# Projection stage of an encoder layer: x turned by the host, the RMS root applied to the output columns, two output buffers, tiles 0 and 1 multiplied while the weights arrive

## The chip, the cores and the metric

One NeuronCore of a Trainium2 chip. The metric is the time of one execution of the whole program on the device, in microseconds; lower is better. Work that the host does on the inputs before the launch is not in it.

## What is computed

A hybrid encoder layer in fp32 for 1024 + 512 tokens (12 tiles of 128), model width 1024: input projection, windowed attention (heads A), dense attention with normalised and rotated q and k (heads B), output projection, expert-choice mixture of 16 experts, a gated embedding. The change is in the first stage:

```python
def rmsnorm(x, g):
    xf = x.astype(jnp.float32)
    r = lax.rsqrt(jnp.mean(xf * xf, axis=-1, keepdims=True) + EPS)
    return (xf * r).astype(x.dtype) * g

h = rmsnorm(x, g_attn[i])
proj = h @ w_in[i]                       # (tokens, 1024) @ (1024, 1536)
qa, ka, va, qb, kb, vb = jnp.split(proj, splits, axis=-1)
# heads B: q = rope(rmsnorm(q, gq)), k = rope(rmsnorm(k, gk)), per head of 64
```

## The kernel before

`project_inputs` (L169) runs the stage; attention of the sample tiles follows. Every fp32 operand of a product is split into a high part (rounded to the PE's fp32r, by ScalarE, "ACT") and a low part (the remainder, by VectorE, "DVE"), and a product is three matmuls: high x high, high x low, low x high. The weights' 1536 columns are three chunks c of 512, held in one PSUM buffer `p_out` of three banks: chunk 0 and the first 128 columns of chunk 1 are q and k of heads B, then k of heads A, v of both, and chunk 2 is q of heads A. A tile is 3 chunks x 8 blocks of the depth x 3 = 72 matmuls of 512 columns.

Weights come in 8 blocks of 768 KB through a ring of three (`load_w`, L237), which waits for `w_lo_made` of three blocks before. ACT makes `w_hi` (L380), DVE `w_lo` (L482).

For each tile of x (512 KB): ACT squares and sums it (L330), GpSimd ("POOL") makes the root (L300 to L311), DVE multiplies x by root and by the gain row `g_all` (L417), PE turns it in eight 128 x 128 blocks into `p_xT` (L510), ACT and DVE split it (L336, L422). `p_xT` takes two PSUM banks, `p_qk` two, the bias rows `p_rows` one, `p_out` three: eight, which is all.

After a tile's products its columns are processed (`post_middle` and `post`): ACT squares q/k of B (L341) and copies v (L344) once chunk 1 is done, DVE sums per head (L433), POOL takes the power (L313, L315), DVE multiplies (L436), applies gains and rotation (L442 to L459), ACT and DVE split q and k (L351 to L360, L461 to L472). PE then turns them with the identity in six rounds of four 128 x 128 blocks (L553) into `p_qk` (two slots), ACT copies each round out (L373) to `qT` or `kT`, and SP's queue stores v, qT (1 MB) and kT (512 KB) in DRAM (L257 to L263). `qT` and `kT` have one buffer each: the first copy of a tile waits for `q_stored` of the tile before, the fifth for `k_stored`.

The order of each engine is written out by hand. PE, per tile t: chunk 0 of tile t - 1, turn x of tile t, chunk 1 of tile t - 1, two rounds of q turns of tile t - 2, chunk 2 of tile t - 1 with the other four rounds between its blocks. As `p_out` is one buffer, a chunk of tile t may begin only when DVE and ACT have read that chunk of tile t - 1:

```python
pe.wait_ge(dve_step, (t - 1) * V_STEPS + (V_NORM, V_KA_LO, V_QA_LO)[c])
if c == 1:
    pe.wait_ge(act_step, (t - 1) * A_STEPS + A_V)
```

Tile 0 is multiplied block by block while the weights arrive (`first_product`, L513), with chunk 1 to 3 of one block together; tile 1 follows after it.

The relative bias of heads A (`BiasRows`): PE looks the table up (L157) at the start, DVE adds (L161), and ACT issues one DMA (L166) after its last `w_hi`, which writes the eight rows 128 times, shifted, to `rel_d` in DRAM (2 MB, from 8 partitions). SP reads it back near the stage's end (`ahead.load_consts`).

SP's queue, per step: load x of a tile (waits until the slot is squared and normalised), then the three stores of the tile three before, each waiting for its copies.

Of the kernel before, what the change touches and what calls it, by code (L numbers as in the profile page):

```python
# [13 lines left out]
P = 128  # L14
# [125 lines left out]
class BiasRows:  # L140


    def __init__(self, a):
        self.table, self.hot = a.sb("table", [BUCKETS, HEADS]), a.sb("hot", [BUCKETS, REL])
        self.outside, self.rows = a.sb("outside", [HEADS, REL]), a.sb("rows", [HEADS, REL])
        self.p_rows = a.ps("p_rows", [HEADS, REL])
        self.landed, self.looked, self.added, self.stored = (
            a.sem(n) for n in ("bias_landed", "bias_looked", "bias_added", "bias_stored"))
# [20 lines left out]
def project_inputs(nc, kept, unit, x, w_in, g_attn, gqk, rope, rel_bias, hot, outside, qT_d, kT_d, v_d, rel_d, ahead):  # L169


    RING = 3
    with ExitStack() as ctx:
# [5 lines left out]
        g_all = sb("g_all", [P, D])  # L179
        gqk_s = sb("gqk_s", [P, 2, HD])  # L180
        nhalf = sb("nhalf", [P, HEADS + KV])
        eps = sb("eps", [P, HEADS + KV])
        x_sb = sb("x", [P, 2, D])
        cs = sb("cs", [P, TILES, 2 * HD])
        sq = sb("sq", [P, 2, D], mybir.dt.bfloat16)
        ss = sb("ss", [P, 2, 1])
        mean = sb("mean", [P, 2, 1])
        rinv = sb("rinv", [P, 2, 1])
        xn, xn_r = a.sb_both("xn", [P, 2, D])
# [25 lines left out]
        x_landed, cs_landed = sems("x_landed", 2), sem("cs_landed")  # L215
        squared, meaned, rooted, normed = sem("squared"), sem("meaned"), sem("rooted"), sem("normed")
        xT_made, h_hi_made, h_lo_made, mm_done = sem("xT_made"), sem("h_hi_made"), sem("h_lo_made"), sem("mm_done")
        act_step, dve_step, pool_step = sem("act_step"), sem("dve_step"), sem("pool_step")
# [9 lines left out]
        qkb, qa = p_out[:, 0:QK_B], p_out[:, 2 * BANK:QKV]  # L228
        ka = p_out[:, QK_B:QK_B + KV * HD]
        vba = p_out[:, QK_B + KV * HD:2 * BANK]  # L230
# [5 lines left out]
        def _(sp):  # L236
# [5 lines left out]
            sp.dma_start(x_sb[:, 0, :], x[0:P, :]).then_inc(x_landed[0], 16)  # L242
            sp.dma_start(g_all[:], g_attn.partition_broadcast(P)).then_inc(g_landed, 16)
            load_w(0)
            load_w(1)
            sp.dma_start(x_sb[:, 1, :], x[P:2 * P, :]).then_inc(x_landed[1], 16)
            load_w(2)
            bias.load(sp, rel_bias, hot, outside)
            sp.dma_start(gqk_all[:].rearrange("p a d -> p (a d)"), gqk.partition_broadcast(P)).then_inc(gqk_landed, 16)
            for k in range(3, KC):  # L250
                load_w(k)
# [13 lines left out]
            def load(t, s):  # L265
                row = sp.snap(t * P)
                sp.wait_ge(squared, t - 1)
                sp.wait_ge(normed, t - 1)
                sp.sem_inc(sp_turn, 1)
                sp.dma_start(x_sb[:, s, :], x[bass.ds(row, P), :]).then_inc(x_landed[s], 16)  # L270

            load(2, 0)
            sp.dma_start(cs[:], rope.rearrange("(t p) n -> p t n", p=P)).then_inc(cs_landed, 16)
            with sp.Fori(1, TILES // 2 - 1) as i:
                for k in range(2):
                    load(i * 2 + k + 1, 1 - k)
                    store(i * 2 + k - 2, k)
            load(TILES - 1, 1)
# [3 lines left out]
            store(TILES - 4, 0)  # L282
# [8 lines left out]
        def _(pool):  # L291
            unit.make(pool)
            pool.memset(nhalf[:], -0.5).then_inc(pool_step, 1)
            pool.memset(eps[:], EPS).then_inc(pool_step, 1)
            pool.wait_ge(pool_step, 2)


            for t in range(2):
                pool.wait_ge(squared, t + 1)
                pool.tensor_tensor(mean[:, t, :], ss[:, t, :], eps[:, 0:1], ALU.add).then_inc(meaned, 1)  # L300
                pool.wait_ge(meaned, t + 1)
                pool.tensor_tensor(rinv[:, t, :], mean[:, t, :], nhalf[:, 0:1], ALU.pow).then_inc(rooted, 1)
# [3 lines left out]

            def pair(t, s):
                pool.wait_ge(squared, t + 1)
                pool.tensor_tensor(mean[:, s, :], ss[:, s, :], eps[:, 0:1], ALU.add).then_inc(meaned, 1)
                pool.wait_ge(meaned, t * 2 - 1)  # L310
                pool.tensor_tensor(rinv[:, s, :], mean[:, s, :], nhalf[:, 0:1], ALU.pow).then_inc(rooted, 1)  # L311
                pool.wait_ge(dve_step, (t - 2) * V_STEPS + V_SUM)
                pool.tensor_tensor(meanh[:], ssh[:], eps[:], ALU.add).then_inc(meaned, 1)  # L313
                pool.wait_ge(meaned, t * 2)
                pool.tensor_tensor(rinvh[:], meanh[:], nhalf[:], ALU.pow).then_inc(pool_step, 1)  # L315

            with pool.Fori(0, TILES // 2 - 1) as i:
                for k in range(2):
                    pair(i * 2 + k + 2, k)
            for t in (TILES - 2, TILES - 1):  # L320
                pool.wait_ge(dve_step, t * V_STEPS + V_SUM)
                pool.tensor_tensor(meanh[:], ssh[:], eps[:], ALU.add).then_inc(meaned, 1)
                pool.wait_ge(meaned, TILES + t + 1)
                pool.tensor_tensor(rinvh[:], meanh[:], nhalf[:], ALU.pow).then_inc(pool_step, 1)

        @block.scalar
        def _(act):
            def square(t, s):
                act.wait_ge(x_landed[s], (t - s) * 8 + 16)
                act.activation(sq[:, s, :], x_sb[:, s, :], ACT.Square, scale=D ** -0.5, accum_out=ss[:, s, :]).then_inc(squared, 1)  # L330

            def high(t, s, first):
                act.wait_ge(xT_made, t + 1)
                if not first:
                    act.wait_ge(mm_done, (t - 1) * 3)
                act.activation(h_hi[:, s, :, :], p_xT[:], ACT.Copy).then_inc(h_hi_made, 1)  # L336

            def post_middle(t, s, second):

                act.wait_ge(mm_done, t * 3 + 2)  # L340
                act.activation(sqh[:], qkb, ACT.Square, scale=HD ** -0.5).then_inc(act_step, 1)  # L341
                if not second:
# [3 lines left out]
            def post(t, first):  # L346

                if not first:
# [3 lines left out]
                               ka.rearrange("p (h d) -> p h d", d=HD).unsqueeze(2).broadcast_to([P, KV, 2, HD]),  # L352
                               ACT.Copy).then_inc(act_step, 1)
                act.wait_ge(mm_done, t * 3 + 3)
                act.activation(q_hl[:, 0:HEADS, 0, :], qa.rearrange("p (h d) -> p h d", d=HD), ACT.Copy,
                               scale=SCALE).then_inc(act_step, 1)
# [1961 lines left out]
```

## Time and profile before

| | |
|---|---|
| median of 3 runs | 1571.12 us (1570.65 to 1572.77) |
| the profiled execution, its own time | 1573.29 us |
| its span, first to last instruction | 1571.5 us |
| PE busy | 1443.1 us (92%) |
| DVE, ACT, POOL busy | 932.7, 722.7, 180.0 us |
| mean granted clock of PE | 0.959 of full speed |
| the projection, until attention's first matmul | 0 to 274 us |

The profile gives, per engine, when each instruction began, how long it was busy and what ended the idle time before it. A matmul's busy time is longer than its share, since matmuls overlap: the distance between the starts of two of them is what one costs.

### The profile page before, as it was taken

How to read it: one execution, taken by the hardware profiler on the slowest of the kernel's cores; microseconds unless marked ns; L12 is line 12 of the kernel's file. 1: busy time of each engine (PE TensorE's matmuls, PEld its weight loads, DVE VectorE, ACT ScalarE, POOL GpSimd, SP SyncE). 2: the span in 40 equal slices, each digit the busy share in tenths (PEclk: the TensorE clock that was granted, in tenths of full speed). 3: DMA queues.
4: the chain of work that ended last, by engine and by line, in shares of the span. 5: the costliest groups of instructions: out<-in, count | busy, mean ns of one | idle time of the engine just before them, and what ended most of it. 6: DMA issues, size and time to landing. Idle time of an engine off the chain costs nothing. (4 is left out here: it accounts for less than half of the span.)

```text
span 1571.5 us, 21444 instructions
## 1 busy us (share of the span) xinstructions
PE 1443.1 (92%) x7320; PEld 1016.3 (65%) x7320; DVE 932.7 (59%) x1324; ACT 722.7 (46%) x1157; POOL 180.0 (11%) x240
## 2 busy tenths in 40 slices
PE   5899998899999889699998799999999999959997
PEld 4778887555566555378887556666666666637885
DVE  5444443667777677533256856776676776644544
ACT  4244433666677567522222544544544444433332
POOL 1111111000000000100001211121121121021110
PEclk9899999799999979899998889999999999979999
DMA  8533353511112243254342847788778778681331
GB/s 263 101 116 114 113 184 115 203 67 65 65 65 66 95 171 118 76 207 139 129 147 96 299 148 254 255 270 272 256 253 263 259 255 268 236 252 68 134 135 67
DMA packets 81983, 261.53 MB, mean 166 GB/s; under 512 B 7648, under 2 KB 37472, under 8 KB 66568
## 3 DMA queue, kind: packets, MB, share of 16 engines
q1 hardware_dynamic: 73728, 233.55, 41.4%
q0 software_dynamic: 7168, 25.17, 6.9%
q10 hardware_dynamic: 1032, 2.10, 1.2%
q8 instruction: 32, 0.52, 0.1%
q14 instruction: 23, 0.19, 0.0%
HBM read 194.20 MB, written 66.58 MB: 166 GB/s over the span
## 5 line engine op out<-in xcount | busy, mean ns | idle before, releaser
L1836 DVE TENSOR_TENSOR moe_w_lo<-ring,moe_w_hi 128x2048 fp32r<-128x2048 f32 x96 | 220.3, 2296 | 157.7 <-ACT moe_w_hi L1775 157.6
L1775 ACT ACTIVATE moe_w_hi<-ring 128x2048 fp32r<-128x2048 f32 x96 | 183.6, 1914 | 202.6 <-PE moe_p_g L1958 122.3
L1486 PE MATMUL mix_p_big<-kept_out_w,mix_m_hi 128*128 128x512 f32 x384 | 126.2, 410 | 4.6 <-DVE mix_m_lo L1361 2.4
L537 PE MATMUL proj_p_out<-proj_w_hi,proj_h_hi 128*128 128x512 f32 x264 | 110.4, 418 | 8.4 <-DVE proj_qn L436 8.4
L1966 PE MATMUL moe_p_gu<-ring,moe_xT_r 128*64 128x512 f32 x512 | 116.9, 598 | 0.0
L537 PE MATMUL proj_p_out<-proj_w_hi,proj_h_lo 128*128 128x512 f32 x264 | 105.3, 399 | 0.0
L537 PE MATMUL proj_p_out<-proj_w_lo,proj_h_hi 128*128 128x512 f32 x264 | 105.2, 399 | 0.0
L1034 DVE TENSOR_REDUCE sample_ntop<-sample_p_s 128x1 f32<-128x1024 f32 x64 | 78.2, 1223 | 42.0 <-PE sample_p_s L857 41.2
L871 PEld LDWEIGHTS sample_p_t<-kept_ident_r,sample_probs_r 128*128 128x128 f32 x688 | 73.0, 141 | 23.6 <-ACT sample_probs L972 6.6
L1486 PEld LDWEIGHTS mix_p_big<-kept_out_w,mix_m_hi 128*128 128x128 f32 x384 | 72.8, 195 | 21.4 <-issue 2.6
L871 PE MATMUL sample_p_t<-kept_ident_r,sample_probs_r 128*128 128x128 f32 x688 | 80.2, 246 | 5.0 <-ACT sample_probs L972 2.5
L2208 PE MATMUL tail_p_out<-kept_pg_hi,tail_h_hi 128*128 128x512 f32 x192 | 77.8, 405 | 2.4 <-DVE tail_h_lo L2152 2.4
L972 ACT ACTIVATE sample_probs<-sample_p_s,sample_ntop 128x1024 f32<-128x1024 f32 x64 | 71.5, 1117 | 18.1 <-DVE sample_ntop L1034 17.8
L1486 PE MATMUL mix_p_big<-kept_out_w,mix_m_lo 128*128 128x512 f32 x192 | 77.6, 404 | 0.0
L2208 PE MATMUL tail_p_out<-kept_pg_hi,tail_h_lo 128*128 128x512 f32 x192 | 76.9, 401 | 0.0
L1966 PEld LDWEIGHTS moe_p_gu<-ring,moe_xT_r 128*64 128x64 f32 x512 | 33.9, 136 | 66.1 <-issue 66.1
L2208 PE MATMUL tail_p_out<-kept_pg_lo,tail_h_hi 128*128 128x512 f32 x192 | 76.4, 398 | 0.0
L881 PE MATMUL sample_p_o<-sample_pT_b,sample_vb 128*64 128x512 f32 x256 | 62.9, 606 | 0.8 <-ACT sample_pT_b L959 0.8
L537 PEld LDWEIGHTS proj_p_out<-proj_w_hi,proj_h_hi 128*128 128x128 f32 x264 | 50.2, 190 | 17.7 <-issue 8.5
L1736 POOL DMA_INDIRECT acc_d<-ring,kept_slots x32 | 50.5, 1580 | 96.2 <-DVE ring L1877 91.9
L1966 PE MATMUL moe_p_yr<-ring,moe_hT_r 128*64 128x512 f32 x256 | 58.5, 598 | 0.0
L1725 POOL DMA_INDIRECT ring<-h_d,kept_slots x16 | 21.4, 1334 | 322.8 <-PE moe_p_t L1934 314.9
(303 smaller groups left out, 3154.7 us busy)
## 6 DMA issues: line engine op xcount, KB each, us to landing
ring<-in_w_gate SPq DMA_DIRECT2D x32, 1024.0 KB, 5.5
ring<-in_w_up SPq DMA_DIRECT2D x32, 1024.0 KB, 7.4
ring<-in_w_down SPq DMA_DIRECT2D x32, 1024.0 KB, 5.6
qT_d<-proj_qT SPq DMA_DIRECT2D x12, 1024.0 KB, 3.9
proj_x<-in_x SPq DMA_DIRECT2D x12, 512.0 KB, 4.8
proj_w_raw<-in_w_in SPq DMA_DIRECT2D x8, 768.0 KB, 6.1
kT_d<-proj_kT SPq DMA_DIRECT2D x12, 512.0 KB, 3.9
ahead_q<-qT_d SPq DMA_DIRECT2D x6, 1024.0 KB, 5.0
```

The costliest lines, as they stand in the source:

```text
L537: last = pe.matmul(p_out[:, cols], h[:, s, k, :], w[:, k, cols], start=(k == 0 and n == 0), stop=(k == KC - 1 and n == 2))
L871: last_mm = pe.transpose(p_t[:, bank, b, :].bitcast(F32R), probs_r[:, head % 4, at:at + P], ident_r[:])
L881: mm = pe.matmul(p_o[kv * HD:(kv + 1) * HD, :, :], v, pT[:, b, kv, :, :], start=(b == begin), stop=(b == end - 1))
L972: act.activation(dst, src, ACT.Exp, bias=ntop[:, s, head:head + 1], accum_out=total[:, s, head:head + 1]).then_inc(exp_done, 1)
L1034: dve.tensor_reduce(ntop[:, s, head:head + 1], p_s[:, head % 2, 0:T], AX.X, ALU.max, negate=True).then_inc(ntop_done, 1)
L1486: mm = pe.matmul(p_out[:, cols], m[:, s, k, :], ww[:, k, cols], start=(k == 0 and n == 0), stop=(k == KC - 1 and n == 2))
L1725: pool.indirect_dma_start(out=xs, out_offset=None, in_=h_d, in_offset=bass.IndirectOffsetOnAxis(ap=slots[:, e:e + 1], axis=0)).then_inc(xs ...
L1736: pool.indirect_dma_start(out=acc_d, out_offset=bass.IndirectOffsetOnAxis(ap=slots[0:rows, col:col + 1], axis=0), in_=y, in_offset=None, c ...
L1775: act.activation(w_hi[:, at % SPLIT], raw[:, at % RAW], ACT.Copy).then_inc(hi_made, 1)
L1836: dve.tensor_tensor(w_lo[:, at % SPLIT], raw[:, at % RAW], w_hi[:, at % SPLIT].bitcast(F32), ALU.subtract).then_inc(lo_made, 1)
L1966: mm = pe.matmul(out[half * R:(half + 1) * R, :], x[:, k0 + k, :], raw[:, (at + half) % RAW, k, :], start=(start and k == 0), stop=(stop a ...
L2208: mm = pe.matmul(p_out[:, s, cols], h[:, s, k, :], ww[:, k, cols], start=(k == 0 and n == 0), stop=(k == KC - 1 and n == 2))
```

## The change

The host gives x a second time as `xT`, turned per tile (128 depth rows x 8 blocks x 128 tokens), and the gain as a [128, 8] array `g_col`. The kernel multiplies the gain into the weights as it splits them and splits `xT` as it is; PE turns no x, `p_xT`, `xn` and `g_all` are gone, and `p_out` has two buffers (six banks). The root of a token is a factor of its output row, so it goes into the scale of the ACT copies and DVE remainders of v, k and q (`rinv` with 1 and with SCALE); for heads B, whose norm would cancel it but for EPS, the EPS term is divided accordingly (the third column of `mean`). x itself is loaded too, for the sum of squares only. The k remainder of heads A becomes two instructions. The weight ring has four slots. PE starts with tile 0 and, from the third block on, tile 1's first three blocks between, then the rest of tile 1; it waits for the readers of tile t - 2 instead of t - 1. The bias look-up shares the bank of `p_qk` slot 0 and moves behind the turns of tile 0, its addition behind the post-processing of tile 1 on DVE, and the store of `rel_d` behind that of tile 1 on ACT. SP asks for xT and x two tiles ahead and stores the tile before the current one.

```diff
-    def look_up(self, pe):
+    def look_up(self, pe, emptied, count):
         pe.wait_ge(self.landed, 48)
+        pe.wait_ge(emptied, count)
...
-    RING = 3
+    RING = 4
+    FEED = 3
...
-        p_xT = a.ps("p_xT", [P, KC, P])
-        p_out = a.ps("p_out", [P, QKV])
+        p_out = a.ps("p_out", [P, 2, QKV])
         p_qk = a.ps("p_qk", [P, 2, 4, P])
-        bias = BiasRows(a)
+        bias = BiasRows(a, p_qk[0:HEADS, 0].rearrange("p a c -> p (a c)"))
...
+            load_xT(0, 0)
+            sp.dma_start(g_col[:], g_attn).then_inc(g_landed, 16)
+            load_w(0)
+            load_w(1)
+            load_xT(1, 1)
+            load_w(2)
+            load_w(3)
+            load_x(0, 0)
+            load_w(4)
+            load_w(5)
+            load_x(1, 1)
+            load_w(6)
+            load_w(7)
+            sp.dma_start(gqk_all[:].rearrange("p a d -> p (a d)"), gqk.partition_broadcast(P)).then_inc(gqk_landed, 16)
             sp.dma_start(cs[:], rope.rearrange("(t p) n -> p t n", p=P)).then_inc(cs_landed, 16)
+            load_xT(2, 0)
+            bias.load(sp, rel_bias, hot, outside)
+            load_xT(3, 1)
+            load_x(2, 0)
+            load_x(3, 1)
+            store(0, 0)
+
+            def step(u, s):
+                load_xT(u + 2, s)
+                load_x(u + 2, s)
+                store(u - 1, 1 - s)
...
         @block.gpsimd
...
+            def root(t, s):
                 pool.wait_ge(squared, t + 1)
+                pool.tensor_tensor(mean[:, s, :], ss[:, s, :].broadcast_to([P, 3]), by[:], ALU.mult).then_inc(scaled, 1)
+                pool.wait_ge(scaled, t + 1)
+                pool.tensor_tensor(mean[:, s, :], mean[:, s, :], plus[:], ALU.add).then_inc(meaned, 1)
...
+                pool.tensor_tensor(rinv[:, s, :], mean[:, s, 0:2], nhalf[:, 0:2], ALU.pow).then_inc(rooted, 1)
...
         @block.scalar
         def _(act):
+            def high(t, s):
+                act.wait_ge(xT_landed[s], (t - s) * 8 + 16)
+                if not isinstance(t, int) or t >= 2:
+                    act.wait_ge(mm_done, (t - 1) * 3)
+                act.activation(h_hi[:, s, :, :], xT_sb[:, s], ACT.Copy).then_inc(h_hi_made, 1)
...
+            def high_w(k):
+                act.wait_ge(w_landed[k % RING], 16 * (k // RING + 1))
+                act.activation(w_hi[:, k, :], w_raw[:, k % RING, :], ACT.Copy, scale=g_col[:, k:k + 1]).then_inc(w_hi_made, 1)
...
-                act.activation(v_sb[:, s, :], vba, ACT.Copy).then_inc(act_step, 1)
+                act.activation(v_sb[:, s, :], vba(s), ACT.Copy, scale=rinv[:, s, 0:1]).then_inc(act_step, 1)
...
+            high(0, 0)
+            act.wait_ge(g_landed, 16)
             for k in range(KC):
                 if k == 2:
+                    high(1, 1)
+                high_w(k)
+            square(0, 0)
+            square(1, 1)
+            post_middle(0, 0)
+            post(0, 0)
+            high(2, 0)
+            post_middle(1, 1)
+            copy_out(0)
+            post(1, 1)
             bias.store(act, rel_d)
...
+            def step(t, s, last=False):
+                square(t, s)
                 if not last:
+                    high(t + 1, 1 - s)
+                post_middle(t, s)
+                copy_out(t - 1)
+                post(t, s)
...
         @block.vector
...
+            def low_w(k):
+                dve.wait_ge(w_hi_made, k + 1)
+                dve.scalar_tensor_tensor(out=w_lo[:, k, :], in0=w_raw[:, k % RING, :], scalar=g_col[:, k:k + 1],
+                                         in1=w_hi[:, k, :].bitcast(F32), op0=ALU.mult,
+                                         op1=ALU.subtract).then_inc(w_lo_made, 1)
...
+            low(0, 0)
+            dve.wait_ge(g_landed, 16)
             for k in range(KC):
                 if k == 2:
+                    low(1, 1)
+                low_w(k)
+            post(0, 0)
+            low(2, 0)
+            post(1, 1)
+            bias.add(dve)
...
         @block.tensor
...
+            def first_products():
                 pe.wait_ge(h_lo_made, 1)
                 for k in range(KC):
                     pe.wait_ge(w_lo_made, k + 1)
                     for c in range(QKV // BANK):
+                        chunk(0, c, k, k + 1)
+                    fed = k - 2
+                    if 0 <= fed < FEED:
+                        if fed == 0:
+                            pe.wait_ge(h_lo_made, 2)
+                        for c in range(QKV // BANK):
+                            chunk(1, c, fed, fed + 1)
+                for c in range(QKV // BANK):
+                    chunk(1, c, FEED, KC)
...
-                pe.wait_ge(dve_step, (t - 1) * V_STEPS + (V_NORM, V_KA_LO, V_QA_LO)[c])
+                pe.wait_ge(dve_step, (t - 2) * V_STEPS + (V_NORM, V_KA_LO, V_QA_LO)[c])
...
+            def step(t, s):
+                product(t, s, 0)
+                product(t, s, 1)
+                transpose_qk(t - 1, 0, 2)
+                product(t, s, 2, spread(t - 1))
+
+            first_products()
             pe.wait_ge(unit.ready, 1)
+            transpose_qk(0, 0, 2)
+            product(2, 0, 0, spread(0))
+            bias.look_up(pe, qk_copied, 6)
+            product(2, 0, 1)
+            transpose_qk(1, 0, 2)
+            product(2, 0, 2, spread(1))
+            step(3, 1)
             with pe.Fori(2, TILES // 2) as i:
                 for k in range(2):
+                    step(i * 2 + k, k)
+            transpose_qk(TILES - 1)
```

## Rows read from the trace of the kernel before

**Rows 1.** The page, busy us (share of the span) and instructions.
```profile
PE 1443.1 (92%) x7320; PEld 1016.3 (65%) x7320; DVE 932.7 (59%) x1324; ACT 722.7 (46%) x1157; POOL 180.0 (11%) x240
```

**Rows 2.** Windows: us, busy of each engine, granted clock, DMA share, GB/s.
```profile
0.00:16.00 16.00, 3.03 (x11) 1.17 (x11) 7.18 (x5) 8.83 (x9) 3.96 (x15) 1.00 0.84 305
44.50:48.50 4.00, 3.98 (x10) 3.13 (x10) 3.86 (x8) 1.28 (x3) 0.00 (x0) 0.50 0.47 50
91.40:111.04 19.64, 19.64 (x106) 16.09 (x105) 9.76 (x15) 8.52 (x17) 2.90 (x4) 1.00 0.34 114
82.39:86.34 3.95, 3.95 (x16) 3.21 (x16) 1.54 (x2) 1.63 (x3) 2.17 (x2) 0.57 0.00 0
```

**Rows 3.** Timeline of the start: start, us, engine, line, operation, what ended the idle.
```profile
4.55 1.06 ACT L330 ACTIVATE proj_sq<-proj_x 128x1024 bf16<-128x1024 f32 x1 [2.55 <-DMA proj_x<-in_x]
...
8.32 1.49 ACT L380 ACTIVATE proj_w_hi<-proj_w_raw 128x1536 fp32r<-128x1536 f32 x1 [2.62 <-DMA proj_w_raw<-in_w_in]
9.84 3.65 DVE L482 TENSOR_TENSOR proj_w_lo<-proj_w_raw,proj_w_hi 128x1536 fp32r<-128x1536 f32 x2 [1.84 <-ACT proj_w_hi L380]
...
14.19 1.87 PE L157 MATMUL proj_p_rows<-proj_hot,proj_table 32*8 32x512 f32 x2 [4.82 <-DMA proj_outside<-in_outside]
...
20.00 0.63 PE L521 MATMUL proj_p_out<-proj_w_hi,proj_h_hi 128*128 128x512 f32 x1
...
21.28 0.47 PE L521 MATMUL proj_p_out<-proj_w_hi,proj_h_hi 128*128 128x512 f32 x1
...
30.45 1.76 DVE L482 TENSOR_TENSOR proj_w_lo<-proj_w_raw,proj_w_hi 128x1536 fp32r<-128x1536 f32 x1 [0.63 <-ACT proj_w_hi L380]
```

**Rows 4.** TensorE's timeline after tile 0.
```profile
44.52 0.77 PE L537 MATMUL proj_p_out<-proj_w_hi,proj_h_hi 128*128 128x512 f32 x1 [8.39 <-DVE proj_qn L436]
```

**Rows 5.** TensorE's timeline around one turn of x.
```profile
71.76 0.79 PE L510 MATMUL proj_p_xT<-kept_ident_r,proj_xn_r 128*128 128x128 f32 x8
72.39 0.47 PE L537 MATMUL proj_p_out<-proj_w_hi,proj_h_hi 128*128 128x512 f32 x1
72.70 0.40 PE L537 MATMUL proj_p_out<-proj_w_lo,proj_h_hi 128*128 128x512 f32 x1
72.93 0.39 PE L537 MATMUL proj_p_out<-proj_w_hi,proj_h_lo 128*128 128x512 f32 x1
```

**Rows 6.** Groups by line, 0 to 430 us: busy us, mean ns, idle before.
```profile
L422 DVE TENSOR_TENSOR proj_h_lo<-proj_p_xT,proj_h_hi 128x1024 fp32r<-128x1024 f32 x12 | 14.7, 1224 | 49.3 <-ACT proj_h_hi L336 49.3
...
L336 ACT ACTIVATE proj_h_hi<-proj_p_xT 128x1024 fp32r<-128x1024 f32 x12 | 12.3, 1024 | 51.5 <-PE proj_p_xT L510 51.5
```

**Rows 7.** Timeline near 80 us: SP's queue, ScalarE, TensorE.
```profile
68.29 4.80 SPq L270 DMA_DIRECT2D proj_x<-in_x  x1
...
79.84 1.06 ACT L330 ACTIVATE proj_sq<-proj_x 128x1024 bf16<-128x1024 f32 x1 [6.22 <-DMA proj_x<-in_x]
...
82.39 0.54 PE L553 MATMUL proj_p_qk<-kept_ident_r,proj_q_hl 128*128 128x128 f32 x4 [2.07 <-ACT proj_qT L373]
```

**Rows 8.** Timeline, tile 11's post-processing: first and last instruction.
```profile
258.05 0.71 ACT L341 ACTIVATE proj_sqh<-proj_p_out 128x640 f32<-128x640 f32 x1 [9.76 <-PE proj_p_out L537]
...
267.85 0.42 DVE L472 TENSOR_TENSOR proj_k_hl<-proj_qg,proj_k_hl 128x256 fp32r<-128x256 f32 x1
```

**Rows 9.** The bias store, and DMAs beside it; issues end with us to landing.
```profile
28.93 0.55 ACTq L166 DMA_DIRECT2D rel_d<-proj_rows  x1
...
q10 hardware_dynamic: 1032, 2.10, 1.2%
...
q10 hardware_dynamic: 73, 0.15, 46.7%
...
v_d<-proj_v SPq DMA_DIRECT2D x1, 128.0 KB, 19.1
...
kT_d<-proj_kT SPq DMA_DIRECT2D x1, 512.0 KB, 12.8
```

**Rows 10.** DMA issued in a quiet stretch, window 125:130.
```profile
qT_d<-proj_qT SPq DMA_DIRECT2D x1, 1024.0 KB, 3.9
```

More of the change, by code:

```diff
@@ L317, in _ @@
-            with pool.Fori(0, TILES // 2 - 1) as i:
-                for k in range(2):
[L319 to L324, printed above, removed]
+            root_heads(0, 0)
@@ L328, in square @@
             def square(t, s):
                 act.wait_ge(x_landed[s], (t - s) * 8 + 16)
[L330 to L338, printed above, removed]
+                if not isinstance(t, int) or t >= 1:
+                    act.wait_ge(squared, t)
@@ L342, in post_middle @@
-                if not second:
+                act.activation(sqh[:], qkb(s), ACT.Square, scale=HD ** -0.5).then_inc(act_step, 1)
+                act.wait_ge(rooted, t + 1)
+                if not isinstance(t, int) or t >= 2:
                     act.wait_ge(v_stored[s], (t - s) * 8)
-                act.activation(v_sb[:, s, :], vba, ACT.Copy).then_inc(act_step, 1)
-            def post(t, first):
-                if not first:
+                act.activation(v_sb[:, s, :], vba(s), ACT.Copy, scale=rinv[:, s, 0:1]).then_inc(act_step, 1)
@@ L349, in post @@
+            def post(t, s):
+                if not isinstance(t, int) or t >= 1:
                     act.wait_ge(qk_round, (t - 1) * 6 + 6)
@@ L383, in _ @@
-            bias.store(act, rel_d)
-            high(1, 1, True)
-            square(2, 0)
-            post_middle(0, 0, True)
-            post(0, True)
-            def tile(t, s, first, second, last=False):
-                high(t, s, False)
-                if not last:
-                    square(t + 1, 1 - s)
-                post_middle(t - 1, 1 - s, second)
-                copy_out(t - 2, second)
-                post(t - 1, first)
-            tile(2, 0, False, True)
-            tile(3, 1, False, False)
@@ L513, in first_product, with chunk @@
-            def first_product():
+            PASSES = ((h_hi, w_hi), (h_hi, w_lo), (h_lo, w_hi))
+            def chunk(s, c, first, last, after=None):
+                cols = slice(c * BANK, (c + 1) * BANK)
+                for k in range(first, last):
+                    for n, (h, w) in enumerate(PASSES):
+                        mm = pe.matmul(p_out[:, s, cols], h[:, s, k, :], w[:, k, cols],
+                                       start=(k == 0 and n == 0), stop=(k == KC - 1 and n == 2))
+                    if after and k < KC - 1:
+                        after(k)
+                if last == KC:
+                    mm.then_inc(mm_done, 1)
@@ L529, in product, with transpose_qk @@
                     pe.wait_ge(h_lo_made, t + 1)
-                pe.wait_ge(dve_step, (t - 1) * V_STEPS + (V_NORM, V_KA_LO, V_QA_LO)[c])
+                pe.wait_ge(dve_step, (t - 2) * V_STEPS + (V_NORM, V_KA_LO, V_QA_LO)[c])
                 if c == 1:
-                    pe.wait_ge(act_step, (t - 1) * A_STEPS + A_V)
-                cols = slice(c * BANK, (c + 1) * BANK)
-                for k in range(KC):
-                    for n, (h, w) in enumerate(((h_hi, w_hi), (h_hi, w_lo), (h_lo, w_hi))):
-                        last = pe.matmul(p_out[:, cols], h[:, s, k, :], w[:, k, cols],
-                                         start=(k == 0 and n == 0), stop=(k == KC - 1 and n == 2))
-                    if after and k < KC - 1:
-                        after(k)
-                last.then_inc(mm_done, 1)
-            def transpose_qk(t, first, begin=0, end=6):
+                    pe.wait_ge(act_step, (t - 2) * A_STEPS + A_V)
+                chunk(s, c, 0, KC, after)
+            def transpose_qk(t, begin=0, end=6):
+                first = isinstance(t, int) and t == 0
                 if begin == 0:
                     pe.wait_ge(dve_step, t * V_STEPS + V_KB_LO)
+                if isinstance(t, int) and t == 1 and begin == 0:
+                    pe.wait_ge(bias.added, 1)
                 for r in range(begin, end):
```

242 lines of the change are left out of this document (98 added, 144 removed).

## The prediction

> **What bounds the kernel now.** The page first: TensorE (PE) is busy 92% of the span [rows 1]; so time comes out of PE's own work or its pauses. The change touches the projection alone, the first 274 us. The table of windows then tells what kind of stage it is: from 91.40 to 111.04, one token tile, PE is busy 19.64 of 19.64 us at a granted clock of 1.00 and every other engine for half or less [rows 2]. Here a faster VectorE or ScalarE buys nothing; only instructions taken off PE do. Last, PE's timeline gives the pauses: nothing useful before about 16 us [rows 3], 8.39 us waiting for L436 after the first tile [rows 4], and 2.07 us waiting for a copy at 80.3 [rows 7]. Each is followed by matmuls at the lower clock: granted 0.50 from 44.5 to 48.5, 0.57 from 82.39 to 86.34 [rows 2].
>
> **The change, part by part.** Units first. At the full clock a 512-column matmul follows the last by 0.233 us, so a tile's 72 take 16.8 us. Eight turns of x take 0.63 us (71.76 to 72.39), and the matmul behind them comes 0.08 late (72.39 to 72.70, against 0.23): 0.71 us [rows 5]. What is left of 19.64 after 16.8 and two such groups (x, and the first eight of q) is four groups of four turns at 0.35. At the lower clock (1.2 instead of 2.4 GHz) a matmul takes 0.427 us (20.00 to 21.28 holds three), 0.194 more [rows 3]; the table's 1.00 for the first 16 us [rows 2] is no evidence, since no record of the clock shows a change before 36 us, and these intervals do.
>
> *Turns of x go.* Ten of twelve stand in PE's dense stretch: 10 x 0.71 = 7.1 us gained. The other two stood in pauses.
>
> *The start.* x's 512 KB were landed by 4.55, the first weights by 8.32, with 512 KB of the gain row between them [rows 3]. That broadcast becomes a few KB: 1.25 MB in 3.8 us becomes 0.75 MB in about 2.3, so weights 0 are there near 6.8. x turned needs only copy 1.02 and subtract 1.22 [rows 6], done by 6.9. Then w_hi 1.49 and w_lo 1.8 [rows 3]: PE starts near 10.1 instead of 16.0. Bounds: 9.7, and 11.7 if the weights are no earlier. The cold start costs as before: about twelve matmuls at the lower clock, 2.3 us. Gain 5.9. The multiply by g_col rides on instructions that exist; the scalar form of w_lo I cost at 0.05 us, hidden behind PE.
>
> *Weights.* From block 2 on PE has 18 matmuls (4.2 us) per block for three blocks, so it reaches block 7 of tile 0 at 10.1 + 2.3 + 90 x 0.233 = 33.4. By then 8 MB are to be moved (eight blocks, x and xT of two tiles): at the 305 GB/s of the first 16 us [rows 2], counted from 1.2, that is 27.5, and with w_hi and w_lo 30.8. Before, with a ring of three, the last w_lo ended at 32.2 [rows 3]. Both are in time: hidden, by one to three us.
>
> *The pause after tile 0.* Tile 1 fills it: first products end at 10.1 + 2.3 + 144 x 0.233 = 46.0. Post-processing of a tile takes 10.2 us from the end of its second chunk to the last q/k remainder (258.05 to 268.27) [rows 8]; tile 0's second chunk ends near 34.9, so it is done by 45.2 plus 0.15 for the split k remainder. High and low parts of tile 2 (1.02 + 1.22) end at 46.6, PE wants them at 46.7 after its first turns. I allow 0.4 us. Gained: 8.4 of waiting, 9 matmuls at the lower clock (1.8), less 0.4: 9.8.
>
> *The look-up* moves from PE's idle start into the stream: 1.87 us cold [rows 3], 0.9 at the full clock. Lost 0.9.
>
> *The stall at 80 us.* x of tile 4 was issued at 68.29 and squared at 79.84; the copies queued behind that square on ScalarE held PE [rows 7]. Now a load is asked a tile ahead and x is squared off PE's path. Gained: 2.07, and of the 3.95 us at 0.57 about half, 1.9: 4.0.
>
> Sum so far: 7.1 + 5.9 + 9.8 - 0.9 + 4.0 = 25.9 us.
>
> *The bias store, moved.* This is the cost. ScalarE issued it at 28.93, in a quiet time for DMA. Now ScalarE issues it after post(1). My timeline: product(2,0) 46.7 to 53.8, look-up, product(2,1) to 60.3; post(1) ends on VectorE near 56.5, bias.add takes it to 57.2; the store goes out at 57.2, between the stores of tiles 0 and 1. It is 1032 packets, 73 in 3 us: 42.4 us long, on 47% of the DMA engines' time, that is half of the engines all the time [rows 9]. Everything that SP's queue moves meanwhile is late: v of tile 0, 128 KB, landed 19.1 us after its issue, kT of tile 0 (issued at 65.73) 12.8 us, against 3.9 for eight times v's bytes in a quiet stretch [rows 9, 10]. Before, only these few hung behind it. Now tile 1's do: qT goes out at 64.5 and by v's row lands at 64.5 + 19.1 + 2.1 (for eight times the bytes I add half of the 3.9 that they take in a quiet stretch) = 85.7. ScalarE's first copy of tile 2 must wait for it, and PE wants that copy at 81.3: 5.0 us idle and 1.8 of lower clock. Behind it goes kT, issued at 67.7. In many small packets it ends with the bias store or soon after: 57.2 + 42.4 + 4 (SP's own packets between, again qT's 3.9) = 103.6; with two copies and four splits on ScalarE (2.8) and two remainders on VectorE (1.0) tile 3's turns can begin at 107.4. PE, 6.8 us late, wants them at 98.1 + 6.8 = 104.9: 2.5 idle and again 1.8. Bounds: nothing, if SP's packets pass quickly, and 17 us, if the loads of tile 5 and qT of tile 2, queued behind kT, hold ScalarE once more. I take 5.0 + 1.8 + 2.5 + 1.8 = 11.1, because v's row is the nearest: the same queue, the same store beside it, mid-life.
>
> The Trainium skill ("DMA: Bandwidth & Descriptors", Queues, rings and completion order) says that a DMA engine goes round the queues it has work for, packet by packet. By that rule a small transfer beside the bias store would lose a packet's time, not 15 us, and this part would cost nothing; v's 19.1 us speaks against it, and the measurement decides.
>
> *Extra xT loads* (512 KB per tile): steady DMA share was 0.34 [rows 2]; it rises by a sixth of a tile's traffic or so and hides under 18.9 us of PE. ScalarE and VectorE lose nothing that matters: they were half idle. *After the stage* all waits are relative to its end; the last tile's post-processing has the same order, 0.15 us longer.
>
> Net: 25.9 - 11.1 = 14.8 us. The profiled execution took 1573.29 (span 1571.5), 2.2 above the median 1571.12; against the first the forecast is 1558.5, on the median's scale **1556.3**.
>
> **Rivals.**
> A. *The bias store does no harm* (the skill's rule, or the late transfers have slack). For it: ScalarE has 19 us per tile and needs 8. Against: rows 9. Time 1571.1 - 25.9 = 1545.2.
> B. *It does more harm*: 12 to 17 us, SP's queue blocked behind kT, so that loads of tile 5 and the next qT are late too. For it: the issue at 68.29 itself took 4.80 us [rows 7], so the ring was full. Time 1557 to 1562.5.
> C. *Slower than before*: PE begins on cold weights and the clock does not rise while they arrive. Then 144 - 12 = 132 matmuls cost 0.194 more: 25.6 us, time 1581.9. It decides once more than about 76 of them (14.8 / 0.194) run at the lower level beyond the twelve. For it: the first dozen did. Against: in the same stage before, the clock rose at 21.3, while weights were still arriving.
> D. *The overlap does not do what it says*: PE starves for weights. It needs w_lo(7) after 33.4; each us beyond is a us lost. If the feed were 4 us late: 1560.3.
>
> **How the numbers follow.** Chances: forecast 0.55 (1551 to 1559), A 0.23, B 0.15, C 0.02, D 0.05. The two sides of the start's bounds, 0.4 and 1.6 us, widen either. From A's lower edge to B's upper: 1544.5 to 1562. What this measurement can tell from no change is 0.2%, 3 us; of the cases only C is on the other side, and about 0.01 of the rest ends within 3 us. So faster 0.97, same 0.01, slower 0.02.
>
> **What would show it.** Right: first matmul near 10; no PE wait over 1 us between 10 and 80; tile period 18.9; x turns gone; the ACTq store of rel_d near 57 with SP landings of 12 to 20 us behind it; a PE wait for ScalarE's q copy near 81, a second, for the last k remainder, near 105; projection's last product about 15 us earlier. Wrong: no PE wait between 60 and 110 (A); a clock of 0.5 beyond 20 us (C); waits for w_lo in the first 46 us (D); two waits of over 10 us together (B).

## The result, and the profile after

The kernel before took 1571.48 us (median of 5 runs, 1570.65 to 1572.77), the changed kernel 1559.66 us (5 runs, 1556.75 to 1563.71): a ratio of 0.9917, 95% interval 0.9904 to 0.9929, so 13.0 us less (11.2 to 15.1). The forecast was 1556.3, with a range of 1544.5 to 1562.0; its likeliest case alone was to take 1551 to 1559. The profiled execution took 1559.1 us, span 1557.1.

The page first: busy time and instructions, beside [rows 1].

```profile
PE 1429.2 (92%) x7224; PEld 1006.1 (65%) x7224; DVE 919.7 (59%) x1324; ACT 725.8 (47%) x1157; POOL 183.3 (12%) x257
```

The 96 matmuls that are gone are the turns of x (12 tiles of eight blocks). PE is busy 13.9 us less, the span is 14.4 us shorter. The windows say where (columns as in [rows 2]):

```profile
0.00:16.00 16.00, 5.72 (x17) 4.59 (x18) 8.59 (x6) 9.60 (x7) 1.20 (x14) 1.00 0.88 354
36.00:46.00 10.00, 9.84 (x49) 8.07 (x49) 7.63 (x14) 4.49 (x9) 2.01 (x2) 1.00 0.04 13
80.00:100.00 20.00, 8.80 (x40) 6.91 (x39) 4.21 (x8) 2.75 (x5) 2.16 (x2) 0.66 0.67 133
120.00:139.00 19.00, 19.00 (x99) 15.74 (x98) 9.36 (x18) 9.11 (x17) 3.24 (x5) 1.00 0.43 152
```

PE works from 10.28 on, and from 36 to 46, where it waited 8.39 us before [rows 4], it is busy 9.84 of 10 us. The steady stretch is still all PE's. And from 80 to 100 PE is busy for 8.80 of 20 us, at a granted clock of 0.66: a new hole. TensorE's timeline at the first product, at the hole, at a second short wait, and at the first matmul of the next stage (start, busy us, and in brackets the idle time before it and what ended it):

```profile
10.28 0.76 PE L550 MATMUL proj_p_out<-proj_w_hi,proj_h_hi 128*128 128x512 f32 x1 [10.28 <-DVE proj_w_lo L461]
...
91.73 0.75 PE L595 MATMUL proj_p_qk<-kept_ident_r,proj_q_hl 128*128 128x128 f32 x4 [11.20 <-ACT proj_qT L419]
...
110.75 0.87 PE L595 MATMUL proj_p_qk<-kept_ident_r,proj_q_hl 128*128 128x128 f32 x8 [0.36 <-DVE proj_k_hl L515]
...
258.16 0.55 PE L895 MATMUL sample_p_s<-ahead_ka,ahead_q 128*128 128x256 f32 x1 [1.95 <-PEq L175]
```

The last of these stood at 273.99 before: 15.8 us are gained when the projection ends, of which 14.4 are left at the end of the program. The other 1.4 went in stages that the change does not touch; single executions of one kernel differ by more than that (1556.75 to 1563.71).

What PE waited for stands in ScalarE's timeline. Its copies of qT and kT may not overwrite what is not yet stored:

```profile
55.88 0.55 ACTq L167 DMA_DIRECT2D rel_d<-proj_rows  x1
...
81.57 0.47 ACT L390 ACTIVATE proj_v<-proj_p_out,proj_rinv 128x256 f32<-128x256 f32 x1 [2.38 <-DMA v_d<-proj_v]
91.08 1.08 ACT L419 ACTIVATE proj_qT<-proj_p_qk 128x512 fp32r<-128x512 f32 x2 [9.04 <-DMA qT_d<-proj_qT]
...
106.61 1.09 ACT L419 ACTIVATE proj_kT<-proj_p_qk 128x512 fp32r<-128x512 f32 x2 [11.62 <-DMA kT_d<-proj_kT]
```

The bias store went out at 55.88. SP's queue beside it:

```profile
58.08 0.35 SPq L268 DMA_DIRECT2D proj_x<-in_x  x1
58.78 4.34 SPq L274 DMA_DIRECT2D v_d<-proj_v  x1
64.15 3.62 SPq L277 DMA_DIRECT2D qT_d<-proj_qT  x1
68.09 4.32 SPq L280 DMA_DIRECT2D kT_d<-proj_kT  x1
72.71 9.15 SPq L260 DMA_DIRECT2D proj_xT<-in_xT  x1
```

In the table of DMA issues, the last number of which is us to landing, qT of 64.15 and kT of 68.09:

```profile
qT_d<-proj_qT SPq DMA_DIRECT2D x1, 1024.0 KB, 26.9
...
kT_d<-proj_kT SPq DMA_DIRECT2D x1, 512.0 KB, 38.4
```

The same 1 MB of qT landed 3.8 us after its issue at 49.6, before the store went out. So the shape of the forecast is there: an earlier start, no pause after tile 0, none of the old stall near 80, and a hole behind the moved bias store. But waits of 11.20 and 0.36 us stand where waits of 5.0 and 2.5 were forecast.

### The profile page after: what moved, and what is told of

It reads as the page before. It is cut to its first block and busy times, and to the rows that moved or that the text cites. A ratio compares the mean times of both kernels' runs of the same rounds, so it can differ in the third digit from the quotient of the medians.

```text
span 1557.1 us, 21333 instructions
## 1 busy us (share of the span) xinstructions
PE 1429.2 (92%) x7224; PEld 1006.1 (65%) x7224; DVE 919.7 (59%) x1324; ACT 725.8 (47%) x1157; POOL 183.3 (12%) x257
## 5 line engine op out<-in xcount | busy, mean ns | idle before, releaser
L550 PE MATMUL proj_p_out<-proj_w_hi,proj_h_hi 128*128 128x512 f32 x288 | 118.5, 411 | 10.4 <-DVE proj_w_lo L461 10.3
L550 PE MATMUL proj_p_out<-proj_w_hi,proj_h_lo 128*128 128x512 f32 x288 | 113.9, 395 | 0.0
L550 PE MATMUL proj_p_out<-proj_w_lo,proj_h_hi 128*128 128x512 f32 x288 | 113.7, 395 | 0.0
L550 PEld LDWEIGHTS proj_p_out<-proj_w_hi,proj_h_hi 128*128 128x128 f32 x288 | 54.9, 190 | 20.9 <-issue 10.3
L550 PEld LDWEIGHTS proj_p_out<-proj_w_hi,proj_h_lo 128*128 128x128 f32 x288 | 54.9, 191 | 12.2
L550 PEld LDWEIGHTS proj_p_out<-proj_w_lo,proj_h_hi 128*128 128x128 f32 x288 | 55.0, 191 | 9.5
```

Source lines behind the costliest of these rows:

```text
L550: mm = pe.matmul(p_out[:, s, cols], h[:, s, k, :], w[:, k, cols], start=(k == 0 and n == 0), stop=(k == KC - 1 and n == 2))
```

## The experiments

Each has its own runs of the kernel before on the same chip; ratios are to those. Where an absolute time is compared with 1559.66, the ratio stands beside it. "The changed kernel" is 0.9917 throughout.

**1 and 2. The store's bytes taken away, with and without the change.** The bias rows are written once, 16 KB, instead of once per partition with a shift, 2 MB. These kernels leave out the shift of the bias by query, so they compute another bias than the layer's; only their times are of use here:

```diff
-        act.dma_start(bass.AP(rel_d.tensor, 0, [[REL + P, HEADS], [HEADS * (REL + P) + 1, P], [1, REL]]),
-                      self.rows[:].unsqueeze(1).broadcast_to([HEADS, P, REL])).then_inc(self.stored, 16)
+        act.dma_start(bass.AP(rel_d.tensor, 0, [[REL + P, HEADS], [1, REL]]), self.rows[:]).then_inc(self.stored, 16)
...
-        sp.dma_start(self.bias[:], self.rel_d[:, :, P - 1:P - 1 + SPAN]).then_inc(self.landed, 16)
+        sp.dma_start(self.bias[:], bass.AP(self.rel_d.tensor, P - 1, [[0, P], [REL + P, HEADS], [1, SPAN]])).then_inc(self.landed, 16)
```

In the changed kernel:

> The changed kernel, but the bias rows are stored once (8 rows, 16 KB) instead of 128 times shifted (2 MB); the read-back takes every partition from that one row, so the shift of the bias by query is left out. Theory (the store's packets stand ahead of SP's on half of the DMA engines): the 11.2 us wait of TensorE for the q copy near 80 to 92 us and the one near 110 are gone, with the lower clock behind them; time 1559.7 - 13.5 = 1546. Rival 1 (SP's queue is full of its own traffic, now that xT comes on top of x): the wait stays, 1558 to 1561.

Measured: 1545.21 us, ratio 0.9828 (0.9809 to 0.9848). Between 10.36 and 238 PE has no wait of 0.3 us or more; the next stage begins 13.6 us earlier than in the changed kernel:

```profile
10.36 0.77 PE L549 MATMUL proj_p_out<-proj_w_hi,proj_h_hi 128*128 128x512 f32 x1 [10.36 <-DVE proj_w_lo L460]
...
238.77 0.87 PE L594 MATMUL proj_p_qk<-kept_ident_r,proj_q_hl 128*128 128x128 f32 x8 [2.67 <-DVE proj_k_hl L514]
...
244.54 0.55 PE L894 MATMUL sample_p_s<-ahead_ka,ahead_q 128*128 128x256 f32 x1 [1.96 <-PEq L174]
```

In the kernel before:

> The kernel before with the same cut (one copy of the bias rows stored, the shift left out). Theory: its own stall at 80.3 us came from the same store; it goes, 4.0 us, 1567.5. With e1_tiny this gives what the rest of the change is worth: 21 to 22 us. Rival 1 (the stall at 80 us is SP's late load alone): 1571.5, the 2.07 us wait stays.

Measured: 1570.06 us, ratio 0.9979 (0.9967 to 0.9990). The wait of 2.07 us near 80 is gone (from tile 1 to 260 PE has no wait of 0.3 us or more), the 8.39 us after tile 0 stay:

```profile
43.77 0.77 PE L536 MATMUL proj_p_out<-proj_w_hi,proj_h_hi 128*128 128x512 f32 x1 [8.39 <-DVE proj_qn L435]
...
268.97 0.55 PE L855 MATMUL sample_p_s<-ahead_ka,ahead_q 128*128 128x256 f32 x1 [1.96 <-PEq L172]
```

What follows: the store beside SP's transfers costs the changed kernel 0.9917 - 0.9828 = 0.9% of 1571, 14 us, and the kernel before 3.3 us (the trace says 5.0, of which 0.75 were there before tile 1 began). The old stall near 80 and the new hole have the same cause, the bytes of the store. Without them on either side the change is worth 0.9979 - 0.9828, 24 us.

**3. The store early, otherwise as it is.** The look-up goes behind block 3 of the weights, the add behind block 5, the store before tile 0's q and k are squared:

```diff
+            bias.store(act, rel_d)
...
+                    if k == 3:
+                        bias.look_up(pe)
...
+                if k == 5:
+                    bias.add(dve)
```

> The changed kernel with the bias look-up after block 3 of the weights, its addition after block 5 and its store right behind the last w_hi on ScalarE, near 28 us, as in the kernel before; still 8 partitions, so half of the engines. Theory: the store lasts from 31 to about 72; qT of tile 0, issued near 50, now hangs behind it and lands near 70; the wait moves to the copies of tile 1, near 62 us, and is a little shorter (7 to 10 us with the clock, against 13): 1552 to 1557. Rival 2 (only the moment mattered: in its old place the store falls into a quiet time): no wait over 1 us before 240 us, 1546.

Measured: 1562.89 us, ratio 0.9930 (0.9915 to 0.9946): no better than where the change put it. The store went out at 27.23; the hole moved with it:

```profile
74.08 0.75 PE L597 MATMUL proj_p_qk<-kept_ident_r,proj_q_hl 128*128 128x128 f32 x4 [12.78 <-ACT proj_qT L418]
```

qT of tile 0, issued at 50.19, landed 23.2 us later. The cause holds, the size forecast for it was again too small (7 to 10 us with the clock, against 12.8 of waiting alone), and with it the time (1552 to 1557). Tiles 0 and 1 run without a pause now, and a store that lasts over 42 us found a tile whose q and k were wanted at both times tried: at its old time it hurts as at its new one.

**4. The store over all 16 engines.** The table is widened so that every head's row stands on 16 partitions, and the 2 MB go out as eight DMAs, whose packets come from all 128 partitions:

```diff
+        R, step = P // HEADS, HEADS * (REL + P) + 1
+        for h in range(HEADS):
+            act.dma_start(bass.AP(rel_d.tensor, h * (REL + P), [[HEADS * step, R], [step, HEADS], [1, REL]]),
+                          self.rows[h * R:(h + 1) * R, :].unsqueeze(1).broadcast_to([R, HEADS, REL])).then_inc(
+                              self.stored, 16)
```

> The changed kernel with the look-up made 16 times over (128 rows in PSUM, stationary operand of 128 columns), and the store of 2 MB issued from 128 partitions in eight DMAs of 16 partitions at the same moment, so on all 16 engines. Theory: 64 packets for each engine instead of 129, at about 0.31 us each 20 us instead of 40: done near 80; qT of tile 1 lands by 80 to 82 and kT soon after; TensorE waits 0 to 3 us near 80: 1547 to 1551. Rival 3 (0.31 us per packet is what the DRAM or the source allows in all, not each engine): the store takes 40 us as before on all engines, waits of 10 us or more, 1558 or above.

Measured: 1558.96 us, ratio 0.9908 (0.9892 to 0.9925). The store was over in 13 us, but nothing was won, for another reason. ScalarE's timeline:

```profile
55.79 10.71 ACTq L176 DMA_DIRECT2D rel_d<-proj_rows  x8
66.84 1.06 ACT L388 ACTIVATE proj_sq<-proj_x 128x1024 bf16<-128x1024 f32 x1 [12.83 <-issue]
```

Issuing the eight took ScalarE 10.71 us, and PE then waited 8.84 us for the copies behind them (70.71). Neither theory on record had this: the time is that of the rival, the reason is another.

**5. The wide store, early, on SP's queue.** As 4, with look-up and add as in 3, and the eight DMAs issued by SP, which has nothing else to do then:

```diff
             load_x(3, 1)
+            bias.store(sp, rel_d)
             store(0, 0)
```

> The changed kernel with three things moved: the 128-row look-up behind block 3 of the weights, its addition behind block 5, and the 2 MB store (eight DMAs of 16 partitions) on SP's queue near 28 us, between the loads of x and the first store of v, where neither ScalarE nor SP has anything urgent. Theory: as in e3_wide the store takes about 13 us on all 16 engines, so it is over near 45, before qT of tile 0 goes out near 50; SP's issuing blocks no engine; TensorE waits for no copy: 1545 to 1547, as e1_tiny, with the computation whole. Rival: something else of the feed waits now (v or x of tile 2 behind the store): a wait near 45 to 60 us, 1550 or above.

Measured: 1546.17 us (5 runs, 1544.02 to 1550.70), ratio 0.9825 (0.9801 to 0.9848). The issues took SP 10.90 us and no one waited for it; from 10.10 to 238 PE has no wait of 0.3 us or more:

```profile
29.77 10.90 SPq L175 DMA_DIRECT2D rel_d<-proj_rows  x8
40.78 1.42 SPq L283 DMA_DIRECT2D v_d<-proj_v  x1
```

The full 2 MB are moved, and the time is that of experiment 1, which moved 16 KB. It beats both kernels: by its ratio it is 27 us under the kernel before, and 0.9917 - 0.9825, 14 us, under the changed one. Three things differ from the changed kernel at once: the spread over the partitions, the moment, and the queue. Experiment 3 shows that the moment alone is not enough, and experiment 4 that the spread alone is not, with ScalarE issuing. The wide store on SP's queue at the later moment, and the narrow one in pieces, were not tried.

**6. Is it SP's backlog, or the engines?** The forecast's error was still open: qT took 26.9 us, not 21.2. In the changed kernel it is issued behind x of tile 4 and v of tile 1. Here x's load stands behind the stores:

```diff
                 load_xT(u + 2, s)
-                load_x(u + 2, s)
                 store(u - 1, 1 - s)
+                load_x(u + 2, s)
```

> The change, with one line moved on SP's queue: in each step the load of x stands behind the three stores instead of ahead of them, so that in the step beside the bias store x of tile 4 (512 KB, issued at 58.08 in the changed kernel) no longer stands ahead of v and qT of tile 1. In steady tiles nothing depends on it. Theory: the first wait came out 11.2 us instead of the 5.0 that were forecast, because qT found SP's queue already full of x and v packets. Then v is issued in 0.4 to 1.5 us instead of 4.34, qT lands 20 to 22 us after its issue instead of 26.9, PE waits 4 to 7 us near 81 to 87 instead of 11.2, and the second wait near 105 comes back at 2 to 5 us, since kT still ends with the bias store; the time is 1554 to 1559, that is 1 to 6 us less than the changed kernel. Rival: the eight engines of the bias store give SP's packets a fixed trickle and qT's own 1 MB is what takes long, or qT lands when the store's share changes, whatever is queued ahead: qT still lands after 25 to 28 us, PE waits 10 to 12 us, and the time is that of the changed kernel within 1 us (1559 to 1561).

Measured: 1558.7 us, ratio 0.9901 (0.9882 to 0.9920). The theory fell, the rival stands (qT lands late whatever is queued ahead). SP's queue was free: v had gone out at 54.30, before the store, and qT's issue at 64.18 took 0.33 us instead of 3.62; it landed after 25.9 us all the same, and PE waited 10.23 us. The table of DMA queues in four stretches of this run, 64 to 68, 73 to 77, 80 to 85 and 92 to 96 (packets, MB, time as a share of 16 engines; q10 is the bias store, q1 is SP's):

```profile
q10 hardware_dynamic: 96, 0.20, 47.0%
q1 hardware_dynamic: 72, 0.52, 31.2%
...
q10 hardware_dynamic: 95, 0.19, 46.5%
...
q1 hardware_dynamic: 117, 0.57, 36.6%
q10 hardware_dynamic: 90, 0.18, 23.3%
...
q10 hardware_dynamic: 92, 0.19, 45.9%
q1 hardware_dynamic: 107, 0.16, 11.0%
```

Half of qT's 1 MB went at once, in the first stretch, by the engines that the store does not use. In the second nothing of SP's moved at all, though half of qT and half of kT were waiting. The other half of qT came from 80 on. So what is late is the half of a transfer that belongs to the store's engines, and it is late whether 0 or 640 KB stand ahead of it.

Why the 640 KB made no difference can be read from the records of single DMA packets. Here qT's first packets of 8 KB moved at 65.1, 64 of them by 67.6, and the other 64 from 77.8 on, 12.8 us after the first. In the changed kernel the same gap stands one transfer earlier: half of x of tile 4 moved from 59.1, the other half from 72.8 on (13.7 us later), v's second half from 76.1, qT's from 79.2. So the backlog cost qT 1.4 us (79.2 against 77.8), about what its landing came forward (26.9 to 25.9). The gap was there in the kernel before, in the very transfer that the forecast was scaled from, v of tile 0, issued at 39.33. Its windows 38 to 42, 42 to 52 and 53 to 58, and then 92 to 94 of experiment 6:

```profile
q10 hardware_dynamic: 98, 0.20, 47.0%
q1 hardware_dynamic: 72, 0.07, 4.8%
...
q10 hardware_dynamic: 242, 0.50, 46.5%
...
q10 hardware_dynamic: 114, 0.23, 44.0%
q1 hardware_dynamic: 71, 0.07, 4.9%
...
q10 hardware_dynamic: 45, 0.09, 44.8%
q1 hardware_dynamic: 46, 0.02, 4.2%
```

Half of v went by 42, nothing of it for ten us, the rest after 53 (13.6 us after its first packet), and then beside the store's packets about one to one. In experiment 3 qT's halves began at 51.1 and 65.0. So where SP had nothing under way on the store's engines, its next transfer there began only 12.8 to 14.0 us late (8 KB, 4 KB or 1 KB packets alike), unless the store ran out first, as it did for qT of tile 0 in the kernel before. Why it is this long no run here shows.

**7. One output buffer.** Experiment 1's kernel, with the products waiting for the tile just before, as a single buffer would need:

```diff
-                pe.wait_ge(dve_step, (t - 2) * V_STEPS + (V_NORM, V_KA_LO, V_QA_LO)[c])
+                pe.wait_ge(dve_step, (t - 1) * V_STEPS + (V_NORM, V_KA_LO, V_QA_LO)[c])
...
-                    pe.wait_ge(act_step, (t - 2) * A_STEPS + A_V)
+                    pe.wait_ge(act_step, (t - 1) * A_STEPS + A_V)
```

> e1_tiny (one copy of the bias rows, the shift left out) with TensorE's waits for the readers of p_out set back to tile t - 1, from tile 2 on, so that the second buffer is there but serves tile 1 alone. Theory: only tile 2 notices it: V_NORM of tile 1 is ready near 49.7, TensorE comes at 46: 3 to 4 us of wait and 1 to 2 us of lower clock, nothing in the steady stretch: e1_tiny + 4 to 6 = 1549 to 1551. Rival (the second buffer carries most of the gain): + 10 or more, waits at every tile.

Measured: 1554.92 us, ratio 0.9870 (0.9850 to 0.9890), and one wait:

```profile
50.67 0.77 PE L549 MATMUL proj_p_out<-proj_w_hi,proj_h_hi 128*128 128x512 f32 x1 [4.15 <-DVE proj_qn L476]
```

The next stage begins at 250.25, 5.7 us behind experiment 1 (6.6 by the ratios). The wait came out a little above the 3 to 4 us forecast, and with what the clock adds behind it the cost is at the upper end of the 4 to 6 us. In the steady stretch there is no such wait, so the second buffer brings nothing there.

**8. Tile 1 not fed between the weights.** The changed kernel with FEED = 0, so that tile 1's products all follow tile 0's:

```diff
-    FEED = 3
+    FEED = 0
```

> The changed kernel with FEED = 0: tile 1 is not multiplied between the blocks of tile 0. TensorE then wants w_lo of block 7 at 10.3 + 2.3 + 63 x 0.233 = 27.3; it was ready at 27.2. Theory: the interleaving hides nothing here, the gain comes from the earlier start and the second buffer: no change beyond 1.5 us, 1558.5 to 1561. Rival (the overlap with the weights carries the gain): waits for w_lo of 4 us or more in the first 30 us, 1563 or above.

Measured: 1560.96 us, ratio 0.9915 (0.9894 to 0.9936), that of the changed kernel. PE waits 0.68 us for weights at 26.41 and nowhere else before the hole. (In the profiled execution the weights came later: PE starts at 11.55, 1.3 us later than in the changed kernel, and the last w_lo is done 1.1 us later.)

**9. PE warmed up.** Experiment 5 with 72 matmuls of 128 columns on the identity, from 1.87 us on, while PE has nothing to do:

```diff
+            pe.wait_ge(unit.ready, 1)
+            for n in range(WARM):
+                pe.matmul(p_qk[:, 0, 0, :], ident_r[:], ident_r[:], start=True, stop=True)
             first_products()
```

> e8_early_wide_sp with 72 matmuls of 128 columns of the identity (into a bank that is overwritten later) on TensorE while it waits for the first weights, 2 to 10 us. Theory: the clock has risen when the first product begins, the twelve slow matmuls (2.3 us) go: 1543 to 1544. Rival: the warm-up matmuls run past the moment the weights are ready, or the clock falls between: 1545 to 1547.

Measured: 1549.71 us, ratio 0.9838 (0.9818 to 0.9858), not better than experiment 5, and above both theories. TensorE's timeline:

```profile
1.87 15.62 PE L630 MATMUL proj_p_qk<-kept_ident_r 128*128 128x128 f32 x72 [1.87 <-POOL kept_ident_r L95]
17.29 0.73 PE L562 MATMUL proj_p_out<-proj_w_hi,proj_h_hi 128*128 128x512 f32 x1
...
21.24 0.56 PE L562 MATMUL proj_p_out<-proj_w_hi,proj_h_hi 128*128 128x512 f32 x1
21.64 0.39 PE L562 MATMUL proj_p_out<-proj_w_lo,proj_h_hi 128*128 128x512 f32 x1
```

They took 0.21 us each, twice what was reckoned, so they ran into the products' time, which begins at 17.29 instead of 10.10; the next stage begins 7.3 us later than in experiment 5 (251.31 against 244.04), of which 2 to 5 us are left in the time of the program. And behind them ten products still began at 0.43 us apart, until 21.6. This does not show what a shorter warm-up or one of wide matmuls would bring; that was not tried. At most it can win the 1.7 us that nine slow products cost.

## Why the prediction was right, step by step

The direction, the gains, the harm and its place came as forecast; that the sum came so close is in part luck. Measured at the first matmul of the next stage, the change gained 15.8 us, against 14.8 in the sum; without the store's harm 29.4 (273.99 - 244.54) against 25.9. So the gains were 3.5 us larger than forecast and the harm 2.5 us larger, and the two cancel. The time of the program, 1559.66, is already above the 1551 to 1559 of the likeliest case and in the 1557 to 1562.5 of rival B (by the ratio, 1558.1, it is in both).

*Turns of x*, 7.1 forecast, 9.7 measured. qT's stores of the steady tiles lie 19.63 us apart before (125.66 to 204.17, four intervals) and 18.66 after (115.54 to 190.17, four): 0.97 a tile, not 0.71. The turns themselves are what [rows 5] say. The rest is that the plain products come a little closer: 0.2275 us apart from 136.26 to 148.09 in the changed kernel, 0.2332 in a like stretch before (127.73 to 134.26). Why they do is not settled.

*The start*, 5.9 forecast, 5.7 measured (15.99 to 10.28); nine slow products instead of twelve add 0.6. The scaled forms cost what was allowed or a little more: w_hi 1.57 against 1.49, hidden as forecast.

*Weights hidden*: yes. The last w_lo was done near 27.2, earlier than the 30.8 of the sum, so rival D had six us of room and more. Experiment 8 shows the same from the other side: even without tile 1 between the blocks PE waits only 0.68 us.

*The pause after tile 0*, 9.8 forecast: there is no wait at all, so the 0.4 us allowed were not needed, and 10.2 is the term. Experiment 7 divides it: about 6 us of it are the second buffer's.

*The look-up*, 0.9: it takes 1.02 us at 53.10 in the stream.

*The stall at 80*, 4.0: the wait is gone. But experiment 2 shows that in the kernel before it was the bias store's doing, worth 3.3 us by the ratio and 4.3 by the trace (5.0 less 0.75). Loading x earlier was one way to be rid of it; the store's harm came back through another door. With these figures the gains add up: 9.7 + 5.7 + 0.6 + 10.2 - 1.0 + 4.3 = 29.5.

*Extra loads.* The sum called 512 KB more "a sixth of a tile's traffic"; beside x, qT, kT and v (some 2.1 MB) it is a quarter, and the DMA share rose from 0.34 to 0.43. It hid all the same.

*The bias store*, 11.1 us of harm forecast, 13.6 measured (258.16 - 244.54; 14 by the ratios). This is the step of the prediction that was mis-sized. It was put together from 5.0 + 1.8 near 81 and 2.5 + 1.8 near 105. The first wait was 11.20 us, the second 0.36, and what is left of the 13.6, 2.0, is the lower clock, for which 3.6 were set down: kT landed at 106.5 (103.6 forecast), but PE, already 6 us later than reckoned, came to tile 3's turns only when the work behind kT was all but done. The error lies in scaling v's 19.1 us by bytes in a quiet stretch, "for eight times the bytes I add half of the 3.9". v's 19.1 us were not a rate: its second half began 13.6 us after its first and then took some 4 us (experiment 6). qT had the same kind of gap, and its second half, eight times v's bytes, then needed 11 to 12 us more beside the store (77.8 to 89.4 in experiment 6), where the forecast allowed 2.1 for all the extra bytes. That I had blamed SP's backlog for it was wrong too (experiment 6).

Rival A (no harm) fell by the 11.2 us wait. The Trainium skill ("DMA: Bandwidth & Descriptors", Queues, rings and completion order) has a DMA engine take its queues in turn and switch between them only at the end of a packet, which by that page is some 9 to 17 descriptors and at most 64. From 92 to 94 the counts of experiment 6 look like turns of one to one: 45 packets of the store, 46 of SP's. From 73 to 77 they do not: 95 to none, with SP's packets pending. The gap of 12.8 to 14.0 us is as long as 41 to 44 of the store's packets at 0.31 us. The trace does not tell how many of the profile's packets make one of the page's, so whether a long packet of the page is behind the gap stays open; the loss of one short packet, which the prediction took from the rule, is not what came. Rival A's time, 1545.2, is that of the kernel whose store does no harm: experiments 1 (1545.2) and 5 (1546.2) both reach it.

Rival B (more harm, 12 to 17 us) has the size right: the harm was 13.6, and its sign, waits of over 10 us together, is there, though in one wait and not in two. Its mechanism is only half there. SP's queue was full (an issue of 9.15 us at 72.71), and the loads behind kT were late (x of tile 5, issued at 82.05, landed after 27.2 us), and so was qT of tile 2 (issued at 95.26, landed after 16.9 us), but PE lost no more than 0.36 us by them, and with the backlog gone the hole stayed (experiment 6).

Rival C: the clock rose after nine products; in the projection it fell only in the hole and in the last turns, from 253 on.

## What to carry to other kernels

A long store from few partitions is not a matter of its own queue: here it held back half of every transfer that passed its DMA engines, and moving it in time moved the hole with it. What helped was to spread its source over all partitions, and to issue it from an engine that nobody waits for, since several DMAs in a row block the engine that issues them. A landing time measured beside such a store must not be scaled by bytes before it is known which part of it is a gap. When work is packed closer, look for transfers that the old pauses had hidden: here they took back 14 of 27 us (0.9917 against the 0.9828 of experiment 1).

## What the runs showed of the hardware

- The store's 2 KB packets take 0.31 us when all come from 8 partitions on eight engines, and 0.16 us when they come from 128 partitions on sixteen: 2 MB in 42 us (before) to 49 (changed), or in 13. The first follows from 95 packets in 4 us at 46.5% of 16 engines, the second from 380 of them (0.78 MB) at 93.9% in the like table of experiment 4 (64 to 68). Sizes and targets are the same.
- Beside such a store, a transfer of SP's moved its half on the free engines at once. On the shared engines it began 12.8 to 14.0 us later where SP had had nothing under way there (before, changed kernel, experiments 3 and 6), and from then on the two queues moved about one packet each in turn (45 to 46 in 2 us).
- Eight DMAs of 256 KB in a row took the issuing engine 10.7 us (ScalarE) and 10.9 us (SP), a little less than the 13 us that their packets took in experiment 4.
- Seventy-two matmuls of 128 columns at the start took 0.21 us each, and PE's clock did not rise over them: the products behind them began 0.43 us apart and went to 0.23 only at 21.6.
